# Attention's probabilities times values as 64-column matmuls on the two column halves of the TensorE array

## What is computed

```
def block(args):
    qn, kn, vn, ok = args
    s = jnp.einsum('bqhgd,bkhd->bhgqk', qn, kn) * scale + bias
    s = jnp.where(band & ok[None, :], s, NEG_INF)
    m = jnp.maximum(jnp.max(s, axis=-1, keepdims=True), sink32)
    p = jnp.exp(s - m)
    p = p / (jnp.sum(p, axis=-1, keepdims=True) + jnp.exp(sink32 - m))
    return jnp.einsum('bhgqk,bkhd->bqhgd', p, vn)      # the step that is changed
```

## Time and profile before

| | |
|---|---|
| median of 3 runs | 2013.19 us |
| the profiled execution | 2014.95 us, span 2013.4 us |
| attention stage in it | about 112 to 361 us |
| TensorE busy in the span | 92% |
| mean granted TensorE clock | 0.948 of full speed |

### The profile page before, as it was taken

How to read it: one execution, slowest core, us unless ns; L and a number is a source line. 1 busy time by engine, 2 the same in 40 slices (tenths; PEclk the granted TensorE clock), 3 DMA queues, 4 the chain that set the end, 5 groups by cost and what they waited for, 6 DMA issues and landing times. The chain is left out here.

```text
span 2013.4 us, 29051 instructions
## 1 busy us (share of the span) xinstructions
PE 1847.5 (92%) x9874; PEld 1583.4 (79%) x9874; DVE 1161.9 (58%) x1922; ACT 869.6 (43%) x1536; POOL 472.3 (23%) x454
## 2 busy tenths in 40 slices
PE   7989997999998999999999797996999999999990
PEld 5877775899998878888887796874888888888870
DVE  4256566311111243443334444668999999999977
ACT  4245555311111222222121212335887878787852
POOL 3013223000000120303121101222485533333320
PEclk9989999999999999999898898996999999999995
DMA  6111201222212302012020462327999999999986
GB/s 182 62 46 46 53 22 43 64 84 75 74 63 66 90 22 84 24 43 64 13 73 3 138 201 73 115 87 274 388 389 385 385 384 384 386 391 385 383 311 262
DMA packets 186164, 333.07 MB, mean 165 GB/s; under 512 B 36704, under 2 KB 118144, under 8 KB 185008
## 3 DMA queue, kind: packets, MB, share of 16 engines
q1 hardware_dynamic: 163984, 277.55, 38.7%
q0 software_dynamic: 21296, 53.26, 7.4%
q10 hardware_dynamic: 816, 1.38, 0.4%
HBM read 304.11 MB, written 46.35 MB: 174 GB/s over the span
## 5 line engine op out<-in xcount | busy, mean ns | idle before, releaser
L2305 POOL DMA_INDIRECT y_d<-e_y,e_idxs x32 | 138.4, 4325 | 202.0 <-DVE e_y L2408 186.7
L2379 DVE TENSOR_TENSOR e_Lg<-e_rawg,e_Hg 128x1024 fp32r<-128x1024 f32 x128 | 148.2, 1221 | 6.3 <-ACT e_Hg L2329 6.3
L2379 DVE TENSOR_TENSOR e_Lu<-e_rawu,e_Hu 128x1024 fp32r<-128x1024 f32 x128 | 148.0, 1221 | 0.0
L2379 DVE TENSOR_TENSOR e_Ld<-e_rawd,e_Hd 128x1024 fp32r<-128x1024 f32 x124 | 143.4, 1222 | 0.0
L2329 ACT ACTIVATE e_Hg<-e_rawg 128x1024 fp32r<-128x1024 f32 x128 | 124.9, 1051 | 6.1 <-PE bank L154 6.1
L152 PE MATMUL bank<-r_wH,xH 128*128 128x512 f32 (+1 forms) x288 | 121.3, 421 | 6.3 <-DVE r_wL L1272 3.6
L2329 ACT ACTIVATE e_Hu<-e_rawu 128x1024 fp32r<-128x1024 f32 x124 | 121.0, 1059 | 0.0
L2329 ACT ACTIVATE e_Hd<-e_rawd 128x1024 fp32r<-128x1024 f32 x124 | 120.7, 1050 | 0.0
L154 PE MATMUL bank<-r_wH,xL 128*128 128x512 f32 (+1 forms) x288 | 115.9, 402 | 0.0
L153 PE MATMUL bank<-r_wL,xH 128*128 128x512 f32 (+1 forms) x288 | 115.7, 402 | 0.0
L1034 DVE TENSOR_TENSOR b_wL<-raw,b_wH 128x1024 fp32r<-128x1024 f32 x24 | 29.3, 1223 | 148.4 <-ACT b_wH L1007 148.4
(11 more groups left out here) (399 smaller groups left out, 4839.2 us busy)
## 6 DMA issues: line engine op xcount, KB each, us to landing
e_rawg<-in_w_gate SPq DMA_DIRECT2D x128, 512.0 KB, 11.5
e_rawu<-in_w_up SPq DMA_DIRECT2D x128, 512.0 KB, 9.7
e_rawd<-in_w_down SPq DMA_DIRECT2D x124, 512.0 KB, 11.0
raw<-in_w_in SPq DMA_DIRECT2D x51, 512.0 KB, 3.9
c_Y<-y_d SPq DMA_DIRECT2D x8, 1024.0 KB, 12.2
gate_t<-b_gr_s POOLq DMA_DIRECT2D x8, 528.0 KB, 3.0
m_t<-b_m_s POOLq DMA_DIRECT2D x8, 528.0 KB, 3.4
m_gate<-gate_t POOLq DMA_DIRECT2D x8, 528.0 KB, 4.1
```

Source lines behind the costliest of these rows:

```text
L2305: pool.indirect_dma_start(out=ch.y_d, out_offset=bass.IndirectOffsetOnAxis(ap=idx[:, e % IDX, 1:2], axis=0), in_=y[:], in_offset=None, bou ...
L2379: dve.tensor_tensor(L[kind][:, q], raw[kind][:, q], H[kind][:, q].bitcast(F32), ALU.subtract).then_inc(w_lo[kind], 1)
```

## The change

The stationary operand of `weigh` becomes the value head once, 64 columns, read where the values lie. Each matmul of 512 moving columns becomes two of 256: the even heads' probabilities go with an output on partitions 0 to 63 of bank 6, and the odd heads' with an output on partitions 64 to 127, in the same 256 columns. ScalarE then takes bank 6 out in one copy of 128 partitions x 256 columns. The doubled tile shrinks to the 32 sample tokens' rows. Its copy on GpSimd waits for the sampled product alone and no longer for `weigh`, and TensorE waits for it ahead of line 917 instead of ahead of each phase's first `weigh`.

```diff
-        Vd = sb("a_Vd", [P, NT, 2, HD])
+        Vd = sb("a_Vd", [NS, 2, HD])
...
                 def values(c):
                     if c:
-                        pool.wait_ge(o_mm, c * NB)
                         pool.wait_ge(z_mm, c * Z_PER)
-                    pool.tensor_copy(Vd[:], ch.V[:, :, c * HD:(c + 1) * HD].rearrange("p n (o d) -> p n o d", o=1)
-                                     .broadcast_to([P, NT, 2, HD])).then_inc(vd_done, 1)
+                    pool.tensor_copy(Vd[:], ch.V[0:NS, NB, c * HD:(c + 1) * HD].rearrange("p (o d) -> p o d", o=1)
+                                     .broadcast_to([NS, 2, HD])).then_inc(vd_done, 1)
...
                     act.wait_ge(o_mm, m + 1)
-                    for par in range(2):
-                        r = slice(par * HD, (par + 1) * HD)
-                        act.activation(out[r, c * 2:c * 2 + 2, n * P:(n + 1) * P],
-                                       banks[6][r, :].rearrange("p (r f i) -> p r f i", r=2, f=2)[:, par], ACT.Copy).then_inc(o_out, 1)
+                    act.activation(out[:, c * 2:c * 2 + 2, n * P:(n + 1) * P],
+                                   banks[6][:, 0:2 * P].rearrange("p (f i) -> p f i", f=2), ACT.Copy).then_inc(o_out, 1)
...
-                    if n == 0:
-                        pe.wait_ge(vd_done, c + 1)
                     pe.wait_ge(pt_hi, m + 1)
                     pe.wait_ge(pt_lo, m + 1)
-                    pe.wait_ge(o_out, 2 * m)
+                    pe.wait_ge(o_out, m)
                     for kb in range(0 if n else 1, 2):
-                        mm = pe.matmul(banks[6][:], Vd[:, n - 1 + kb].rearrange("p o d -> p (o d)"), PT[:, kb].rearrange("p g i -> p (g i)"),
-                                       start=(kb == (0 if n else 1)), stop=(kb == 1))
+                        for par in range(2):
+                            mm = pe.matmul(banks[6][par * HD:(par + 1) * HD, 0:2 * P], ch.V[:, n - 1 + kb, c * HD:(c + 1) * HD],
+                                           PT[:, kb, 2 * par:2 * par + 2].rearrange("p f i -> p (f i)"), start=(kb == (0 if n else 1)), stop=(kb == 1))
...
                         pe.wait_ge(cv_in, (c + 1) * (32 * DB))
-                        pe.matmul(b7[:, 0:P], Vd[0:NS, NB].rearrange("p o d -> p (o d)"), ZT[0:NS, 1, :], start=True, stop=False)
+                        pe.wait_ge(vd_done, c + 1)
+                        pe.matmul(b7[:, 0:P], Vd[:].rearrange("p o d -> p (o d)"), ZT[0:NS, 1, :], start=True, stop=False)
```

## The result

The changed kernel takes 1997.53 us (median of 4 runs, 1995.30 to 1998.18), the kernel before 2012.00 us (4 runs, 2009.62 to 2014.44). The ratio is 0.993, 95% interval 0.9917 to 0.9943: faster by 0.57 to 0.83%. The prediction was 1994 us, in a range from 1986 to 2015. The profiled execution took 1997.53 us with a span of 1995.9 us.

The account below looks back on a forecast made before the run. TensorE's list was taken to bound phases 0 to 2, a chain of engines phase 3. Gains 13.9 + 7.3 less 1.9 gave 19.3 us: 1996 from the profiled 2014.95, 1994 by the median; range 1986 to 2015.

Parts of the forecast that it names:

- the staggered halves: Rival: in `weigh` the second column half starts a pass late, 5 slots not 4; 1999 us; 0.19 together with the slow clock.
- the slow clock: Rival: phase 3 at 1.2 GHz throughout, more slow stretches earlier; 2000 us; chance 0.19 together with the staggered halves.
- (a): TensorE's `weigh`: eight 256-column passes run side by side on two column halves, saving 0.86 us, 0.43 in block 0.
- the rival with visible loads: Rival: in `weigh` each pass ends before the next weights load, 2.52 us per `weigh`; 2033 us; chance 0.09.
- (b): Array layout change at the exit from `weigh` to `chunk`: a new gap of 0.10 us, bounds 0 to 0.20.
- The row with 32 columns: Profile row: a 32-column stationary behind a 128-column one starts without a gap; taken as lower bound, 0, for the exit gap.
- (c): Phases 0 to 2: 17 full `weigh` and three of block 0 save 13.9 us; the three of block 4 bring nothing.
- (d): Phase 3: shorter `weigh` and one output copy instead of two save 7.3 us of 11.3; bounds 2 and 11.3.
- The ring: Phase 3 step: `weigh`, out copy, exponentials, `a_PT` copy, next `weigh`; 5.67 us, to shrink by 1.25 us.
- The deduction of 4 us for VectorE and the clock: Phase 3: 2 us for VectorE and 2 us for the clock taken off the 11.3 us, leaving 7.3.
- (e): Clock in phases 0 to 2: one more slow stretch behind the longer `turn_keys` wait loses 1.9 us, bounds 0 to 4.
- All behind attention moves as a block: Stages behind attention: claimed to start earlier and take as long as before, at no cost.

Follow-up runs that it names:

- The kernel with the copy first: Changed kernel with `turn_keys` behind the projection chunk and two phase-3 output banks, plus VectorE copying bank 5 ahead of its maximum in block 1: 1993.23 us.
- second trace of before: The unchanged kernel before, run once more for another trace: 2009.95 us.
- the passes hold the clock: Eight unused 264-column passes added between `weigh` and `turn` in phase 3, from m = 25: 1989.62 us on the changed kernel, 2011.39 on the one before.
- late `turn_keys`: `turn_keys` of block 5 moved behind the projection chunk: 2010.38 us on the kernel before, 1992.30 us on the changed kernel.
- the delay: Changed kernel with one extra ScalarE copy of 128x768 at the start of the branch stage, to start everything behind attention later: 1997.91 us.

## Why the prediction was right, point by point

The mechanism was that of the forecast, and the sum was 1994 for a measured 1997.5 us. By the total alone two rivals lie nearer: the staggered halves (1999) and the slow clock (2000). The trace decides against both: the passes of a pair start 0.007 us apart and 8 passes take 4 slots, not 5; and from `weigh(23)` to the branch stage the granted clock was 0.85, against 0.87 in the first trace of before, and not 1.2 GHz throughout.

(a) The passes. Right: 0.86 us saved in a full `weigh`, by passes in pairs. The passes on one half (2015.69 us, 18 us above the changed kernel, some 1 us of it for two copies) show that this is the overlap: shorter loads and shorter passes without it do not make the kernel faster. Loads of one column half run beside passes of the other, and of its own (passes 0.216 us apart on one half), on the same 128 rows. So the sentence of the Trainium skill ("TensorE: Matmul & The Clock Gate", The mechanism) by which LDWEIGHTS overlaps a running matmul only when the row group differs, by which the rival with visible loads would have come about, does not hold here.

(b) The exit gap. Mis-sized: 0.21 us, not 0.10; the upper bound, 0.20, taken from the gaps at the scores, was right. The row with 32 columns, on which I leaned for the lower bound, was no case of it. In the 17 full steps that is 1.9 us more, of which the shorter first load, which the forecast had at nothing, gives back 17 x 0.05 = 0.9. The Trainium skill ("TensorEngine Tiling (Array Packing)", Key Properties) says that a change of the tiling mode drains TensorE; it gives no length, and the 0.21 us agree with it.

(c) Phases 0 to 2. Forecast 13.9 us. From the table and its counterparts in the other phases, a phase gains 0.28 + 0.39 + 5 x 0.70 + 0 = 4.2 us without slow clock; three phases less `weigh(23)` give 11.9 us, the lower end of the bounds. Block 4 brought nothing, as worked out (m = 12, 9.08 us in both), and 0.70 us as soon as `turn_keys` no longer stood behind it. Not foreseen: in block 1 `weigh(8c + 1)` waits for VectorE's copy of bank 5, so that step gains 0.39, not 0.70. Counted from the start of one `weigh` to the start of the next it is plainer: the 17 steps that the forecast had at 0.76 gain 0.70 each without slow clock, 11.9 us together, and from `weigh(8c)` to `weigh(8c + 1)` it is 6.52 us in both kernels, so the saving in block 0, forecast at 3 x 0.33 us, did not arrive at all. The kernel with the copy first has 6.07 us there.

(d) Phase 3. Forecast 7.3 us of 11.3, measured 7.1 at full clock in both. The ring was read rightly where it rules, but that the sums agree is in part luck, since three kinds of terms were off. The ring's own steps gain 1.55 and 1.58 us (m = 23, 27), not 1.25, since one copy in place of two is worth 0.64, not 0.39. The steps m = 25 and 26 together gain 0.26 us and m = 28 nothing (6.41 to 6.17, 6.25 to 6.23, 6.07 to 6.22), where I had 0, 1.25 and 1.3: ahead of `turn(26)` and `turn(29)` TensorE now waits 1.12 us each for GpSimd's `normalize` (0.25 and 0.26 in the second trace of before), which itself follows VectorE's reciprocal, and from `turn(26)` to `weigh(26)` the sample tokens' products and the scores take 4.0 us in both kernels. And m = 29 and 30, which I had at 2.1 us each at the lower clock, gain 0.07 and 1.57 us in the profiled pair, 0.44 and 0.70 where the passes hold the clock. The deduction of 4 us for VectorE and the clock stood in for that.

(e) The clock. Forecast: 1.9 us lost in phases 0 to 2 and 2 in phase 3, nothing behind. In phases 0 to 2 the profiled pair has 6.8 us at 1.2 GHz before and 3.4 after, so nothing was lost there in this pair. But behind attention the changed kernel loses 0.8 us in the branch stage and 3.2 to 4.3 in retention, with not one instruction changed there. "All behind attention moves as a block" was the step that failed, worth 4 to 5 us, and it is most of what the forecast missed.

The cause of this loss stays open. For the lower clock of phase 3 speaks that the passes which hold the clock there bring branch and retention back to 290.7 and 464.4 us in the changed kernel, and change nothing behind attention in the kernel before (290.7 and 464.9), which did not have the loss. But the amount of slow clock in phase 3 cannot be all of it. The first trace of before has 13.7 us at 1.2 GHz there, as much as the changed kernel's, and no loss (290.7 and 465.5 us). The kernel before with late `turn_keys` has 6.8 us, like the second trace of before, and 468.0 us in retention. The passes on one column half have none, and 467.1 us. In the branch stage the traces fall in two groups: 291.3 to 291.9 us in all seven of kernels with the overlapped `weigh` and no extra passes (291.9 with the delay in it), with 6.8 us at 1.2 GHz that begin within 0.8 us of the stage's start; and 290.6 to 290.7 us in the other seven, with 3.4 us that begin 2.1 to 3.6 us behind it. A second rival, then, is where the stage's start falls between the clock's changes, and the passes move that too. One test of it, the delay, was too small to tell. Every kernel but the one before has one trace only, and runs of one kernel lie 2 to 9 us apart; the medians show that the passes help the changed kernel, not why.

The net of it for the profiled pair: attention ended 21.3 us earlier, branch and retention gave back 4.0, and the span is 17.4 us shorter. The profiled run of before was 3 us above its median, and the medians differ by 14.5 us, against 19.3 forecast: (c) brought 2.0 us less than forecast, the clock in phases 0 to 2 no loss where 1.9 was forecast, and behind attention 4 to 5 us went that the forecast did not have.

## What to carry to other kernels

Where two small outputs need the same moving rows, 64-column matmuls on the two column halves ran fully side by side in float32 here, in both orders in which they were listed; price the change of layout at both ends with the gap that the trace shows at another such change. Read from the order of waits which steps have something fixed behind them (here the keys behind block 4, VectorE's copy behind block 0, GpSimd's `normalize` in four steps of phase 3), since a shorter instruction there only lengthens a wait. And when a change takes work from TensorE in a stage where it idles, look at the clock there and in the stages behind: filling the idle places with matmuls that nobody reads won 7 to 8 us here, half of what the change itself had brought, and nothing in the kernel before. It is worth a run; what it does to the later stages was not explained.

## What was not expected of the hardware

- With all even heads listed first, TensorE starts the odd half's first load 0.013 us behind the even half's, although seven instructions of the even half stand between them in the list (inferred from the pairs, see there).
- On ScalarE a copy of 128 partitions followed by an exponential of 128 costs 0.28 us from start to start; two copies of 64 cost 0.80 us together.
- Stages with the same instructions differed in length by trace: retention 464.4 to 465.5 us in five traces, 467.1 in one and 468.0 to 468.9 in eight.
